# A hybrid encoder on one core: four output tiles' finished rows inside attention's last pair, and the late weight tiles split by two engines

## What is computed

```python
def chunk_attention_prompt(xn, w_qkv, w_out, rel_bias):
    q, k, v = split_qkv(xn, w_qkv)
    ...                                     # 128 query rows against at most 640 keys, masked to the band
    return out @ w_out, k[:, S - rows:], v[:, S - rows:]

hp = hp + yp                                # yp = out @ w_out; the same for the streams
hp = hp + swiglu_ffn(rms_norm(hp, norm_ffn[layer]), ffn_w_gu[layer], ffn_w_down[layer])
```

## Time and profile before

| | us |
|---|---|
| median of 3 executions | 3655.14 (3652.82 to 3660.01) |
| the profiled execution | 3654.89 |
| its span in the trace | 3653.2 |
| TensorE busy | 3420.5 (94%) |
| VectorE / ScalarE / GpSimd busy | 1751.3 / 1258.8 / 1727.5 |
| output projection's wide products, 384 | 67.1 |
| its narrow products, 192 | 37.0 |

### The profile page before, as it was taken

One profiled execution on the slowest core, in us unless ns is written; L12 is line 12 of the kernel. 1 busy time (PEld: TensorE's weight loads), 2 busy tenths in 40 slices (PEclk: granted clock), 3 DMA queues, 4 the chain that ended last, 5 costly groups with the idle time before them and its releaser, 6 DMA issues. The chain is left out here.

```text
span 3653.2 us, 85915 instructions
## 1 busy us (share of the span) xinstructions
PE 3420.5 (94%) x34270; PEld 3166.9 (87%) x34270; DVE 1751.3 (48%) x3059; ACT 1258.8 (34%) x2585; POOL 1727.5 (47%) x1518
## 2 busy tenths in 40 slices
PE   8999878888886999999999999999969999999999
PEld 7999767777775999999999977777749899999998
DVE  6212457766673375454554533333332744545444
ACT  5212444455442132222222334444441322222224
POOL 5444355554551544544445543444336454454554
PEclk9999899999997999999999999999979999999999
DMA  4422101111103111111111234444441111111111
GB/s 149 154 87 86 65 23 38 38 44 42 44 17 114 66 50 40 52 37 49 46 40 49 90 75 107 104 89 102 99 123 31 38 52 45 41 46 40 52 37 69
DMA packets 419823, 234.93 MB, mean 64 GB/s; under 512 B 189587, under 2 KB 393635, under 8 KB 418646
## 3 DMA queue, kind: packets, MB, share of 16 engines
q1 hardware_dynamic: 415970, 216.57, 21.1%
q10 hardware_dynamic: 3572, 14.33, 1.0%
HBM read 188.28 MB, written 47.80 MB: 65 GB/s over the span
## 5 line engine op out<-in xcount | busy, mean ns | idle before, releaser
L2110 PE MATMUL ps<-xs,split 128*128 128x384 f32 x4032 | 739.3, 334 | 0.0
L2030 POOL TENSOR_TENSOR split<-work,split 128x512 fp32r<-128x512 f32 x320 | 409.5, 1290 | 676.1 <-ACT split L2255 676.1
L2110 PEld LDWEIGHTS ps<-xs,split 128*128 128x128 f32 x4032 | 703.6, 188 | 0.0
L2379 DVE TENSOR_TENSOR H<-ps,H 128x1152 f32<-128x1152 f32 x320 | 434.0, 1356 | 495.4 <-PE ps L2124 495.3
L2124 PE MATMUL ps<-split,split 128*128 128x384 f32 x2880 | 554.8, 336 | 11.2 <-DVE split L2453 11.1
L2124 PEld LDWEIGHTS ps<-split,split 128*128 128x128 f32 x2880 | 506.9, 189 | 12.4 <-DVE split L2453 11.7
L1214 PE MATMUL ps<-arena 64*64 64x64 f32 (+2 forms) x8800 | 429.1, 236 | 50.8 <-DVE arena L1640 15.5
L1214 PEld LDWEIGHTS ps<-arena 64*64 64x64 f32 x8800 | 323.5, 136 | 87.1 <-issue 35.1
L2255 ACT CAST split<-work 128x512 fp32r<-128x512 f32 x320 | 194.6, 620 | 585.4 <-PE ps L2110 349.3
L2862 PE MATMUL ps<-xs,split 128*128 128x384 f32 x1656 | 359.8, 354 | 2.6 <-POOL split L2800 2.6
L587 PE MATMUL ps<-mixed,wsplit_mix 128*128 128x384 f32 x1872 | 334.1, 340 | 10.9 <-DVE mixed L799 10.6
(11 more groups left out here) (311 smaller groups left out, 5212.3 us busy)
## 6 DMA issues: line engine op xcount, KB each, us to landing
work<-in_ffn_w_gu SPq DMA_DIRECT2D x168, 256.0 KB, 3.1
work<-in_ffn_w_down SPq DMA_DIRECT2D x88, 256.0 KB, 2.9
work<-in_cache_v SPq DMA_DIRECT2D x64, 256.0 KB, 3.8
work<-in_cache_k SPq DMA_DIRECT2D x256, 64.0 KB, 2.2
rkv_scratch<-lora ACTq DMA_DIRECT2D x24, 576.0 KB, 2.8
stage_mix<-in_rwkv_w_rkv SPq DMA_DIRECT2D x24, 512.0 KB, 3.7
work<-in_attn_w_qkv SPq DMA_DIRECT2D x24, 512.0 KB, 4.1
h_scratch<-H SPq DMA_DIRECT2D x2, 4608.0 KB, 14.5
```

The costliest lines, as they stand in the source:

```text
L2030: pool.tensor_tensor(w[:, 1, :], UNIT_SOURCE[i], w[:, 0, :].bitcast(F32), ALU.subtract).then_inc(u_lo, 1)
L2110: last = pe.matmul(bank(b), w[:, part, k * P:(k + 1) * P], operand[xpart][:, k, :], start=(first and k == 0 and a == 0), stop=(k == 3 and ...
L2379: dve.tensor_tensor(by3(mem.H[:, k, :]), mem.ps[:, DOWN:DOWN + 3, 0:CW], by3(mem.H[:, k, :]), ALU.add).then_inc(added, 1)
```

## The change

1. **Splits by thirds.** S has a third as second argument: a split is 384 columns, in the order S(0..5, third 0) and S(0..2, third 1) in the fill of the pair before the last (among its value products, in slots 7 and 8), S(3, 1) in slot 0 of the last pair, S(4, 1) and S(5, 1) in slot 1, S(6, 0) and S(6, 1) in slot 2, and S(k, 2) in slots 3 to 9. Row 7 follows the last item: thirds 0 and 1 ahead of the last D, third 2 behind it.
2. **F units.** `tail_fill` now gives a list for each slot with F(m, c, k): the three products of tile m, third c, row k for m = 0 to 3, c = 0 and 1, k = 0 to 6, in banks 6 and 7: 56 units, 168 products. 6 or 7 stand in slots 0 to 2, 5 in slots 3 to 8, 3 in slot 9 and 4 around the last D. Tiles 0 to 2 are added to `H` by VectorE, a third at a time (6 additions); for that SP reads the first two thirds of rows 0 to 3 of `H` back early (HE). Tile 3 stays in PSUM.
3. **Projection.** With `early=4` the wide part does row 7 of tiles 0 to 3, then tiles 4 to 7 whole. The rest of `H` is read back by HL.
4. **Weights.** Tiles 1 to 3 are loaded and split by GpSimd's quarters inside the last pair. Tiles 4 to 7 and the two of the feed-forward ("late") are copied by ScalarE to the high part in one operation of 1024 columns (`late_high`), and GpSimd makes the low part in two subtractions of 512 (`late_low`): the first two ahead of the norm, the others among its squares and additions. The tiles' places in SBUF change; two lie in two halves (`TwoHalves`).

```diff
+        if self.early:
+            x_ready(KB - 1)
+            for m in range(self.early):
+                wide(m, KB - 1, KB - 1 if m + 1 < self.early else 0)
+            for m in range(self.early, KB):
+                tile_ready(m)
+                pe.wait_ge(self.left, m - 3 if m < 6 else m - 1)
+                for k in range(KB):
                     wide(m, k)
+            x_ready(KB)
...
+                if p == PAIRS - 1 and u == 2 and c == 1 and k < PAIRS - 2:
+                    unit.append(("S", k, 0))
+                if p == PAIRS - 1 and u == 2 and c == 2 and k in (2, 4, 6):
+                    unit.append(("S", k // 2 - 1, 1))
...
+ADDED_BY = {(0, 3): (LATE + 2,), (0, 4): (LATE + 3,), (0, 7): (LATE + 4,), (1, 7): (LATE + 5,)}
+HIGH_BY = {3: LATE + 2, 4: LATE + 3, 6: LATE + 4, KB: LATE + 5}
...
 def tail_fill():
-    out = [[("S", k)] for k in range(PAIRS - 1)]
-    out[0].insert(0, ("LW", QKV_TILES + 1))
+    n = QKV_TILES
+    last = PAIRS - 2
+    first = [[[("F", 0, c, k)] for k in range(last)] for c in range(2)]
+    rest = [[("F", 0, c, last)] for c in range(2)] + [[("F", m, c, k)] for m in range(1, EARLY_TILES) for c in range(2) for k in range(last + 1)]
+    out = [[[("LW", n + 1), ("HE", 0), ("HE", 1), ("HE", 2), ("S", 3, 1)]] + first[0], [[("S", 4, 1)]] + first[1]]
+    done = 0
+    for j in range(2, NI):
+        more = 7 if j == 2 else 5 if j < NI - 1 else 3
+        out.append(rest[done:done + more])
+        done += more
+    out[1][0] += [("HE", 3)]
+    out[1][3] += [("S", 5, 1)]
+    out[2].insert(0, [("S", last, 0), ("S", last, 1)])
+    for j in range(3, NI):
+        out[j][2] = out[j][2] + [("S", j - 3, 2)]
     for q in range(4):
-        out[q].append(("W", QKV_TILES + 1, q))
-    out[4].append(("LW", QKV_TILES + 2))
-    return out
+        out[q // 2][2 + 2 * (q % 2)].append(("W", n + 1, q))
+        out[2 + q // 2][1 + 2 * (q % 2)].append(("W", n + 2, q))
+        out[4 + q // 2][1 + 2 * (q % 2)].append(("W", n + 3, q))
+    out[1][6].append(("LW", n + 2))
+    out[3][4].append(("LW", n + 3))
+    out[5][4].append(("LW", n + 4))
+    return out, rest[done:]
...
-    out += slot(N, [], []) + [("D", N - 1), ("S", PAIRS - 1)]
+    out += slot(N, [], []) + [key for unit in left_over[:2] for key in unit] + [("S", PAIRS - 1, 0), ("S", PAIRS - 1, 1), ("D", N - 1)]
+    out += [key for unit in left_over[2:] for key in unit] + [("S", PAIRS - 1, 2), ("HL", 0)]
...
+        def late_high(act, n):
+            act.wait_ge(*loaded(n))
+            if n == LATE:
+                items_left(act)
+            elif n == QKV_TILES + KB:
+                act.wait_ge(w_split, 4 * n)
+            act.copy(late_tile(n)[0][:, 0:D], raw(n)).then_inc(w_high, 1)
+
+        def late_low(pool, n):
+            high, low = late_tile(n)
+            pool.wait_ge(w_high, n - LATE + 1)
+            for c in range(2):
+                cols = slice(c * 512, (c + 1) * 512)
+                pool.tensor_tensor(low[:, cols], raw(n)[:, cols], high[:, cols].bitcast(F32), ALU.subtract).then_inc(w_split, 2)
...
+                    pe.wait_ge(ol_ready, SPLIT_NO[k, c])
+                    for a, (w, part) in enumerate(PASSES):
+                        last = pe.matmul(ps[:, GEMM + c, 0:CW], mem.w8[m][w][:, k * P:(k + 1) * P],
+                                         mem.xs[:, part, k, c * CW:(c + 1) * CW],
+                                         start=(k == 0 and a == 0), stop=(m + 1 < EARLY_TILES and k == PAIRS - 2 and a == 2))
...
+                    dve.wait_ge(f_done, 2 * m + c + 1)
+                    dve.tensor_tensor(h, ps[:, GEMM + c, 0:CW], h, ALU.add).then_inc(f_left, 1)
...
                 elif what == "S":
-                    k = N
-                    dve.wait_ge(oh_ready, k + 1)
-                    dve.tensor_tensor(mem.xs[:, 1, k, :], att_out[:, k, :], mem.xs[:, 0, k, :].bitcast(F32), ALU.subtract).then_inc(ol_ready, 1)
+                    k, c = key[1:]
+                    cols = slice(c * CW, (c + 1) * CW)
+                    dve.wait_ge(oh_ready, SPLIT_NO[k, c])
+                    dve.tensor_tensor(mem.xs[:, 1, k, cols], att_out[:, k, cols], mem.xs[:, 0, k, cols].bitcast(F32), ALU.subtract).then_inc(ol_ready, 1)
```

More of the change, by code:

```diff
@@ L255, in tensor, with wide @@
         mem, norm = self.mem, self.norm
-        def wide(m, k):
+        def wide(m, k, first=0):
             for a, (w, part) in enumerate(PASSES):
@@ L306, in scalar @@
             norm.square(act, 0, k)
+            between(k)
         for k in range(3):
@@ L313, in scalar @@
                 norm.hi(act, 0, (3, 4, 6).index(k))
+        between(KB)
         norm.root(act, 1)
@@ L2596, in attention_order @@
             if not (key[0] == "G" and key[2] < 2) and not (key[0] == "W" and key[1] < 3)]
+    last_fill, left_over = tail_fill()
     for p in range(PAIRS):
-        fill = gemm_fill(p + 1) if p + 1 < PAIRS else tail_fill()
-        share = 9.2 if p + 1 < PAIRS else 8
+        fill = gemm_fill(p + 1) if p + 1 < PAIRS else [unit for units in last_fill for unit in units]
         done = 0
@@ L2602, in attention_order @@
             N = NI * p + n
-            upto = min(len(fill), int(len(fill) * (n + 1) / share))
+            upto = min(len(fill), int(len(fill) * (n + 1) / 9.2)) if p + 1 < PAIRS else done + len(last_fill[n])
             extra = []
@@ L2633 @@
 ATTENTION_ORDER, TURN_UNIT = attention_order()
+SPLITS = [key[1:] for key in ATTENTION_ORDER if key[0] == "S"]
+SPLIT_NO = {kc: n + 1 for n, kc in enumerate(SPLITS)}
+ROWS_SPLIT = max(SPLIT_NO[k, c] for k in range(PAIRS - 1) for c in range(3))
 def gemm_unit(p, u, c):
@@ L2822, in _, with between @@
                 elif what == "P":
-                    proj.pool(pool)
+                    late_low(pool, LATE)
+                    late_low(pool, LATE + 1)
+                    def between(t, k):
+                        for n in ADDED_BY.get((t, k), ()):
+                            late_low(pool, n)
+                    proj.pool(pool, between)
                 elif what == "R" and item(N)[0] == "band":
@@ L2866, in _ @@
                         last.then_inc(g_done[b], 1)
+                elif what == "F":
+                    m, c, k = key[1:]
+                    if k == 0:
+                        pe.wait_ge(w_split, 4 * (QKV_TILES + m) + 4)
+                        if m == 0:
+                            for cc in range(3):
+                                evicted(pe, PAIRS - 1, 2, cc)
+                        else:
+                            pe.wait_ge(f_left, 2 * m - 1 + c)
+                    pe.wait_ge(ol_ready, SPLIT_NO[k, c])
[3 more added lines that the diff above has]
+                                         start=(k == 0 and a == 0), stop=(m + 1 < EARLY_TILES and k == PAIRS - 2 and a == 2))
+                    if k == PAIRS - 2 and m + 1 < EARLY_TILES:
+                        last.then_inc(f_done, 1)
                 elif what == "V":
@@ L3244, in __getitem__, with __init__ @@
         return self.parts[key[1]][(key[0],) + key[2:] if len(key) > 2 else (slice(None), slice(None), slice(None))]
+class TwoHalves:
+    def __init__(self, first, second):
+        self.parts = (first, second)
+    def __getitem__(self, key):
+        half, start = divmod(key[1].start, 512)
+        return self.parts[half][:, start:start + key[1].stop - key[1].start]
 def attention_tiles(mem):
```

119 lines of the change are left out of this document (75 added, 44 removed).

## The result

Five executions of the changed kernel have a median of 3633.89 us (3632.05 to 3639.93) against 3655.11 us before (3652.82 to 3660.01, five): 21.2 us less, a ratio of 0.9945 with a 95% interval of 0.9934 to 0.9957. Its profiled execution took 3635.54 us, with a span of 3633.8. One of the ten executions of experiment 8's first run took 6565 us, far from the nine others, and is left out of its median.

The account below looks back on a forecast made before the run. It took each item's chain over the engines to bound the last pair, and TensorE the projection. Terms -29.2 + 2.3 + 3.8 + 0.4 + 0.3 = -22.4 us from 3654.9 gave 3632.5; 8-in-10 range 3618 to 3646.

Parts of the forecast that it names:

- Part 1: Output projection's wide part: 168 products moved out of it, at 0.174 us each, save 29.2 us.
- Part 2: Last attention pair: with fill and splits its ten slots sum to 78.0 us against 75.7, +2.3, at full clock.
- GpSimd's waits: Last pair: GpSimd's waits for loads of weight tiles 1 to 3 cost nothing, bound +2 us.
- Part 3: Pair before the last: nine splits in slots 7 and 8 add 2.7 and 1.1 us, together +3.8.
- Part 4: From the last pair to the projection: last row's splits and tile 4's cost +0.4 us, with a 0.3 stall.
- Part 5: Late weight tiles, projection to feed-forward: all split in time, least margin 1.7 us; norm slightly later, +0.3 us.
- Rival (a): Last pair: splits cost little through overlap, pair near its floor at 66 to 72 us; 3621 in all, chance 0.18.
- Rival (b): Last pair: waits add up through GpSimd's loads, or part runs at half clock; 3638 to 3650 us, chance 0.17.
- (c): Last pair: clock stays at half throughout, pair 115 us long; slower than before at 3670 us, chance 0.04.
- (d): Last pair: moved products push its items back one for one, nothing gained; 3655 us, chance 0.04.

Follow-up runs that it names:

- experiment 8: Changed kernel with the six late tiles split by GpSimd alone, in quarters ahead of the norm: 3647.66 us, when run again 3648.74 us.
- Experiment 2: Changed kernel with row 6's two splits moved from slot 2 to the end of slot 1 of the last pair: last pair 78.89 us against 80.51.
- experiment 4: Changed kernel with all splits moved to ends of slots or behind weighted values, in both pairs: 3626.00 us, ratio 0.9908 to the kernel before.
- version 5: Changed kernel with all those split moves, and GpSimd's splitting of weight tiles 2 and 3 placed later: 3618.28 us, ratio 0.9902 to the kernel before.
- experiment 7: Changed kernel with each F unit cut to one product of 16 columns (384 where it opens a sum), outputs incomplete: last pair 83.81 us against 80.51.
- experiment 3: Changed kernel with the pair before's nine splits put behind the weighted values of its slots 7, 8 and 9, three each: 3637.0 us, one execution.
- experiment 1: Changed kernel with third 2's splits in slots 3 to 9 moved behind the slot's last unit: last pair 75.91 us against 80.51.

## Why the prediction held, and where it did not

3632.5 us were forecast, 3633.9 measured. Its steps, one by one:

- **Part 1** (-29.2): right. The wide part went from 67.1 us of products to 37.7, so 29.4.
- **Part 2** (+2.3, sum 78.0): the last pair is 80.5, +4.8. Nine of the ten slots came within 0.6 us of the slots forecast. The term mis-sized is slot 2, 10.2 instead of 7.4. I had two splits between the evacuations, but not that TensorE's own first two units wait for them (1.88 us), nor that a good part of the slot would run at 1.2 GHz (granted clock 0.67). Experiment 2 shows it: with the splits earlier that slot is 6.05 at clock 1.00. The premise "no hole of more than about 1.5 us, so I take full clock" failed twice: there is a hole of 1.88 us, and the clock fell ahead of it, behind holes of at most 0.99 us. Over the pair it was 0.96.
- The same part's "a third behind the last turn costs 0.4 us" was too small where streams are (slot 5: forecast 7.6, measured 8.2, and 6.8 with the split moved), since two more VectorE operations of the stream stand behind it, one of which took 0.89 us instead of 0.34.
- **GpSimd's waits** (0, bound +2): right for the change, by a margin that experiments 2 and 4 show to be thin: as soon as the splits cost less, TensorE waits 2 and then 6 us, which passes the bound.
- **Part 3** (+3.8): 4.3, near by luck. Slots 7 and 8 got 2.1 and 0.75 longer (2.7 and 1.1 forecast), so slot 9 starts 2.8 us late and not 3.8. Another 1.4, booked at nothing, came in slot 9, which runs partly at half clock (0.81). In both profiles of experiment 8 it did not (slot 9 6.9, the pair 77.2), so that share goes with the clock and not with the splits' places, which cost 2.8. The forecast also counted five splits in slot 7 and two in slot 8; the trace has six and three.
- **Part 4** (+0.4): -0.2. It is 2.60 us to the first product (2.9 forecast), without the stall of 0.3 behind it, against 1.68 and the wait of 1.14 for tile 2 before.
- **Part 5** (+0.3): 0.1. The addition that was to start 0.6 late starts 5.1 us after the last wide product, against 4.9 before; the margins of all tiles held.
- **Rival (a)**, splits nearly free and the pair at its floor, was not what the change did, but what it could have: version 5 has 71.2 us against the forecast 66 to 72. **Rival (b)** had the right kind of extra wait in a smaller size. **(c)** and **(d)** did not come; experiment 7 shows that the clock would have been at 0.66 without fill. Its 84 us don't test the 115 of (c), which had the fill's work in them.

Between the spans the terms of the sum gave -22.4 us and -19.4 came: the last pair +2.5, the pair before +0.5, the way to the narrow part -0.8 and the norm -0.2 against the forecast, and +1.0 which the profiled execution had lost ahead of the stage, where the change touches nothing. The median lies 1.6 below that execution, so it is off by 1.4 only; the 1.6 is scatter between executions, and the sum itself missed by 3.0.

Three versions of one order of work, with hardly any, a third of and the whole fill, had granted clocks of 0.66, 0.86 and 0.96 over the last pair. The Trainium skill ("TensorE: Matmul & The Clock Gate", section "Why this matters for your kernels") says that TensorE kept busy without long holes holds its throughput; the series agrees. Slot 2 of the changed kernel does not: the clock fell there although no hole in slots 0 and 1, 13.5 us long, was over 0.99 us.

## What to carry to other kernels

When a stage is bound by a chain over several engines, its TensorE holes can be filled at no cost in the sum (the clock gives back more than the products take), but every helper operation of the fill has a place in an in-order queue, and its price is mostly that of the place, not its duration: put it behind the operation that frees the bottleneck. Among the turns of the pair before, nine splits cost 2.8 us (4.3 where the clock fell too). Behind the weighted values six of them cost nothing, and the three ahead of a narrow item 1.7, since its evacuation was due at once. When one wait is taken away, look at who waited in its shadow: here GpSimd's normalisation behind a weight load, worth 6 us once the splits were out of the way.

## What the runs showed of the hardware

- Four profiles show the same order in slot 2 with the clock falling at different moments. In the changed kernel it fell 0.4 us into the scores, 1.6 us ahead of the hole, and no hole in the two slots ahead was over 0.99 us. In experiment 3 it fell even ahead of the scores, at the end of a pause of 0.98 us. In experiment 1 and in the second profile of the changed kernel it fell behind the hole of 2.13 us. Six products took 2.29 us at 1.2 GHz instead of 1.3. So the last hole alone doesn't tell when the clock falls; what does is left open by these runs.
- On VectorE a small scaling of 128 x 112 with two SBUF inputs took 0.89 us in slot 5 instead of 0.34, while GpSimd worked beside it. The Trainium skill ("SBUF — State Buffer", section "SBUF: two separate sides") says that such an operation and a GpSimd operation that reads SBUF exclude each other; the trace agrees in this row, and in experiment 1, where the scaling of 128 x 16 behind it took 0.59 us instead of 0.23 beside a GpSimd operation.
